# Norms in token halves at the stage boundaries of a two-block transformer kernel

## What is computed

```python
def first_block(...):
    for l in range(2):
        x = _post_norm(x, _swiglu(_modulate(x, sh1, sc1), ...), g1, 0.5, ...)
        x = _post_norm(x, _token_mixer(_modulate(x, sh2, sc2), ...), g2, 1.0, ...)
        x = _post_norm(x, _swiglu(_modulate(x, sh3, sc3), ...), g3, 0.5, ...)

def _post_norm(x, y, gate, res_w, gain, bias):
    return _layer_norm(ALPHA * x + res_w * (1.0 + gate) * y, gain, bias)

def second_block(...):
    for i in range(2):
        x = x + mixer_i(rmsnorm(x, g_mix[i]))
        x = x + cross_attn(rmsnorm(x, g_xattn[i]), rmsnorm(mem, g_mem[i]), ...)
        x = x + square(relu(rmsnorm(x, g_mlp[i]) @ w_up[i])) @ w_down[i]
```

## Time and profile before

| | |
|---|---|
| median of 3 runs | 3772.74 us (3771.07 to 3775.48) |
| the profiled execution | 3767.59 us, span 3766.3 us |
| mean granted TensorE clock | 0.961 of full speed |
| TensorE busy | 3578.6 us, 95% |
| DVE, ACT, POOL busy | 1759.2, 1234.8, 507.3 us |
| DMA | 373.40 MB, 99 GB/s on average |

### The profile page before, as it was taken

One profiled execution on the slowest core, in us unless ns is written; L12 is line 12 of the kernel. 1 busy time (PEld: TensorE's weight loads), 2 busy tenths in 40 slices (PEclk: granted clock), 3 DMA queues, 4 the chain that ended last, 5 costly groups with the idle time before them and its releaser, 6 DMA issues.

```text
span 3766.3 us, 40780 instructions
## 1 busy us (share of the span) xinstructions
PE 3578.6 (95%) x16716; PEld 2898.0 (77%) x16716; DVE 1759.2 (47%) x3072; ACT 1234.8 (33%) x1670; POOL 507.3 (13%) x433
## 2 busy tenths in 40 slices
PE   8999999899998999999899989988999998999999
PEld 7888767678886888767688876746878887787887
DVE  5544553555444544444533234685543333564332
ACT  2222362332223222462332223234442223343222
POOL 1010121110011010121110011111121111202111
PEclk9999899999998999999899998988999999999999
DMA  6443222134432443211122221100212222222222
GB/s 257 166 148 145 102 86 81 56 123 149 164 135 101 155 158 131 83 46 45 50 105 90 100 73 58 66 12 34 90 62 96 101 101 72 99 75 82 101 92 76
DMA packets 52604, 373.40 MB, mean 99 GB/s; under 512 B 5825, under 2 KB 5953, under 8 KB 9538
## 3 DMA queue, kind: packets, MB, share of 16 engines
q1 hardware_dynamic: 52418, 370.79, 27.3%
HBM read 368.67 MB, written 2.10 MB: 98 GB/s over the span
## 4 chain that ended last, share of the span: by engine, by line
PE 86%; DVE 7%; ACT 4%; issue 2%; POOL 1%; DMA 0%; ACTq 0%; DVEq 0%; SPq 0%; POOLq 0%
PE ps L1215 85%; DVE s_wl L1844 1%; ACT s_wh L1537 1%; DVE s_hl L1838 1%; PE ps L1235 0%; DVE s_xr L1932 0%; ACT L1642 0%; DVE s_tmp L2064 0%; DVE s_hh L1938 0%; ACT s_tmp L1673 0%; DVE s_tmp L2054 0%; POOL s_tmp L2340 0%; ACT s_hh L1537 0%; POOL s_hl L2316 0%; DVE s_sm L2062 0%
## 5 line engine op out<-in xcount | busy, mean ns | idle before, releaser
L1215 PE MATMUL ps<-s_hh,s_wh 128*128 128x512 f32 (+1 forms) x2840 | 1138.7, 401 | 59.8 <-DVE s_hl L1838 32.7
L1215 PE MATMUL ps<-s_hl,s_wh 128*128 128x512 f32 (+1 forms) x2840 | 1120.5, 395 | 0.0
L1215 PE MATMUL ps<-s_hh,s_wl 128*128 128x512 f32 (+1 forms) x2840 | 1119.8, 394 | 0.0
L1844 DVE TENSOR_TENSOR s_wl<-s_stage,s_wh 128x2048 fp32r<-128x2048 f32 (+1 forms) x277 | 628.5, 2269 | 721.7 <-ACT s_wh L1537 721.5
L1537 ACT ACTIVATE s_wh<-s_stage 128x2048 fp32r<-128x2048 f32 (+1 forms) x277 | 519.8, 1877 | 732.6 <-PE ps L1215 621.8
L1215 PEld LDWEIGHTS ps<-s_hh,s_wh 128*128 128x128 f32 (+1 forms) x2840 | 541.8, 191 | 203.5 <-issue 68.9
L1215 PEld LDWEIGHTS ps<-s_hh,s_wl 128*128 128x128 f32 (+1 forms) x2840 | 541.1, 191 | 117.5 <-issue 0.2
L1215 PEld LDWEIGHTS ps<-s_hl,s_wh 128*128 128x128 f32 (+1 forms) x2840 | 542.6, 191 | 113.1 <-issue 2.4
L1215 PE MATMUL ps<-s_ah,s_wh 128*128 128x512 f32 x1216 | 474.4, 390 | 0.0
L1215 PE MATMUL ps<-s_ah,s_wl 128*128 128x512 f32 x1216 | 473.2, 389 | 0.0
L1215 PE MATMUL ps<-s_al,s_wh 128*128 128x512 f32 x1216 | 473.1, 389 | 0.0
(11 more groups left out here) (414 smaller groups left out, 3285.9 us busy)
## 6 DMA issues: line engine op xcount, KB each, us to landing
s_stage<-in_w_ada SPq DMA_DIRECT2D x64, 1024.0 KB, 4.8
s_stage<-in_ffn_w_gate SPq DMA_DIRECT2D x44, 1024.0 KB, 4.8
s_stage<-in_ffn_w_up SPq DMA_DIRECT2D x44, 1024.0 KB, 4.8
s_stage<-in_ffn_down SPq DMA_DIRECT2D x32, 1024.0 KB, 4.8
s_stage<-in_w_up SPq DMA_DIRECT2D x32, 1024.0 KB, 4.8
s_stage<-in_down_m SPq DMA_DIRECT2D x32, 1024.0 KB, 4.7
s_stage<-in_w_in SPq DMA_DIRECT2D x24, 1024.0 KB, 4.8
s_stage<-in_ffn_down SPq DMA_DIRECT2D x16, 768.0 KB, 4.2
```

Source lines behind the costliest of these rows:

```text
L1215: return pe.matmul(out, lhs, rhs, start=start, stop=stop, skip_group_check=True)
L1844: dve.tensor_tensor(m.WL[:, ws, 0:n], m.STAGE[:, j % NS, 0:n], m.WH[:, ws, 0:n].bitcast(F32), ALU.subtract).then_inc(*e.up("dve_w", "w.lo" ...
```

## The change

Tokens 0 to 255 are half 0, tokens 256 to 511 half 1.

- `residual` writes the last product of a stage (the last `down` group, `w_out` of the first block, `wo_x`): of its chunks the last two are kept and done for half 0 and then for half 1. The norm of half 0 is a unit whose small steps are put between the pieces of half 1's products by `tick`; what is left of it comes at the end of them.
- `in_halves` writes the next stage's first three chunks: all three for half 0, with half 1's norm in steps between them, then the rest of that norm, and all three for half 1. So three chunks must be split at once: `NW = 3`. The third slot and eight buffers for squares and the like lie in the upper part of SBUF, which the mixers use for themselves; they give it back and take it by `lend` and `reclaim`. There is one set of `s_ah` and `s_al` left.
- `prefetch` splits a weight chunk as soon as the slot and the stage buffer allow, in place of one chunk ahead at a fixed point. At the start two chunks are split ahead of the first modulation, in place of one.
- `ln_x` goes tile by tile, one per piece of a product. The groups of the feed-forwards are 8, 6 and 8. The rate of `w_ada` chunks is 0.85 in the feed-forwards, 0.3 in the first mixer and 0 in the second; the other weights keep their order.
- The even mixer has three chunks in halves (`w_kiwi`, `w_in_e` 7 and 0) and one more (`w_in_e` 1) ahead of the point at which `ki` must be ready. Where a `g_xattn` norm stands, nothing but names changes. The last feed-forward's end has no norm and stays.

```diff
-FFN_GROUPS = [(0, 8), (8, 8), (16, 6)]
+FFN_GROUPS = [(0, 8), (8, 6), (14, 8)]
...
-NW = 2
+NW = 3
...
+    def prefetch(self):
+
+        while self.stream and self.nsplit < len(self.stream) and self.nsplit in self.issued:
+            j = self.nsplit
+            if self.stream[j][2]:
+                if len(self.tmp.busy.intersection(range(6))) > 4:
+                    break
+                self.nsplit += 1
+                self.ada(j, *divmod(self.stream[j][1], 36))
+                continue
+            ws = [w for w in self.spare_w if w in self.allowed]
+            if not ws:
+                break
+            self.nsplit += 1
+            self.split(j, ws[0])
+
...
+        self.prefetch()
...
+        if self.stream:
+            self.wfree[ch.ws] = event
+            self.spare_w.append(ch.ws)
+            self.prefetch()
+
+    def lend(self, *events):
+
+        self.allowed = {0, 1, 2}
+        self.wfree[2] = list(events)
+        self.tmp.ids += UP
+        for i in UP:
...
-            self.add("low", *self.split(0))
-            self.nsplit = 1
+        self.prefetch()
...
+    def in_halves(self, *work, reclaim=False):
+
+        chs = []
+        for s in (0, 1):
+            if s and self.late:
+                self.drain(self.late)
+                self.late = None
+            if s and reclaim:
+                self.reclaim()
+            for i, (name, idx, product) in enumerate(work):
+                if s == 0:
+                    if i == 0 and self.late:
+                        self.active.append(self.late)
+                    chs.append(self.take(name, idx, ada=False))
+                product(chs[i], s, i == 0)
+                if s:
+                    self.release(chs[i], ("proj", self.pid))
+
...
+        def half(s):
+            yield
+            if s:
+                yield from self.wait_ticks(2)
+            mean = self.banks.take()
+            self.add("ln_mean", sid, acc[0], xv, mean, s)
+            if s:
+                self.tmp.free(acc[0], ("ln.mean", sid, 0), ("ln.mean", sid, 1))
+            sq = [self.tmp.take(UP) for _ in range(4)]
+            self.add("ln_sub", sid, xv, mean, sq, s)
+            self.banks.free(mean, ("ln.sub", sid, NT - 1, s))
+            yield from self.wait_ticks(4 + s)
+            var, y = self.held.take(), self.yr.take()
+            self.add("ln_var", sid, sq, var, y, s)
+            for q in sq:
+                self.tmp.free(q, ("ln.var", sid, s))
+            self.held.free(var, ("rs.v", "ln", sid, s))
+            yield from self.wait_ticks(2)
+            rs = self.banks.take()
+            self.add("ln_rs", sid, y, rs, s)
+            self.yr.free(y, ("ln.rs", sid, s))
+            if nxt:
+                for i in range(0, NT, 2):
+                    q = self.tmp.take(UP)
+                    self.add("ln_h", sid, rs, small, hfree[s], hv, q, s, i)
+                    self.tmp.free(q, ("h.lo", hv, i, s), ("h.lo", hv, i + 1, s))
+                    yield
+                self.banks.free(rs, ("ln.sc", sid, NT - 1, s))
+                if s:
+                    self.active.append(scaled())
+                return
+            sq = [self.tmp.take(UP) for _ in range(4)]
+            self.add("ln_last", l, idx, sid, rs, sq, [v + 1 for v in xv], s)
...
+        def scaled():
+            for n in range(NT):
+                self.add("ln_x", sid, n, small, hv, xv[n] + 1)
+                yield
+            self.small.free(small, *both(None, "x", NT - 1, xv[NT - 1] + 1))
...
+            for i, (name, idx, product) in enumerate(work):
+                ch = self.take(name, idx, ada=gi > 0 or i > 2)
+                product(ch, None)
+                self.release(ch, ("proj", self.pid))
...
+                self.residual([(names["down"][gi], l * 4 + c) for c in range(4)], G, 256, "a", av,
+                              gate[-1] if gate else None, norm)
+                continue
...
+    def residual(self, names, kt, nc, x, ver, gate, norm, order=None, reads=False):
...
+        whole = len(names) - 2
...
+        def tile(c, t, s):
+            n = per * c + t
+            b, pid = self.feat(chs[c], kt, nc, t, x, ver, s, order=order)
+            self.upd(n, xv[n], b, pid, gate, s)
+            if n > per * whole or s is None and n:
+                self.total(kind, *total, n - 1, xv, s)
+            return pid
...
+        for s in (0, 1):
+            for c in range(whole, len(names)):
+                if s == 0:
+                    chs.append(self.take(*names[c], ada=False))
+                for t in range(per):
+                    pid = tile(c, t, s)
+                if s:
+                    self.release(chs[c], ("proj", pid))
+            self.total(kind, *total, NT - 1, xv, s)
+            ends.append(("proj", pid))
+            if s == 0:
+                if reads:
+                    self.hfree = ends
+                units = begin(total)
+                self.active.append(units[0])
+        self.drain(units[0])
+        self.late = units[1]
         if gate:
...
-        self.add("m_begin", l)
-        proj(9, "sq", True)
-        proj(10, "sk")
...
+        self.in_halves(("w_kiwi", 0, keys), ("w_in_e", 7, turn_wi), ("w_in_e", 0, feats("qa", 0, 0)), reclaim=True)
+        proj(1, "qa", 2, 4)
...
-        for i, key in enumerate(("qa", "ka")):
-            for c in range(2):
-                proj(2 * i + c, key, 2 * c, 8 * i + 4 * c)
+        for c in range(2):
+            proj(2 + c, "ka", 2 * c, 8 + 4 * c)
...
-            self.rate = 0.62
-            total = self.ffn("swiglu", "f1%d" % l, ffn1, l, FFN_GROUPS, [2, None], "ln")
...
+            self.rate = 0.85
+            self.ffn("swiglu", ffn1, l, FFN_GROUPS, [2, None], then(l, 0, (l, 3, 4)))
+            self.rate = 0.3 if l == 0 else 0
...
+    def ln_x(sid, n, small, hv, v):
+        AG, AB = m.small(small)[:, 16:24], m.small(small)[:, 24:32]
+        e.wait_ge(both(None, "h.hi", hv, n), both(None, "h.q", hv, n))
+        act.activation(m.XR[:, n, :], m.XR[:, n, :], ACT.Identity, bias=AB[:, n:n + 1], scale=AG[:, n:n + 1]).then_inc(
+            *e.half("act_x", None, "x", n, v))
...
         assert at <= self.BIG
+        self.WH[2], at = self.put("wh2", [P, 2048], self.UPPER, F32R)
+        self.WL[2], at = self.put("wl2", [P, 2048], at, F32R)
+        up, at = self.put("up", [P, 8, S], at)
```

More of the change, by code:

```diff
@@ new lines, in take @@
+    def take(self, name, idx, ada=True):
+        if not self.stream:
+            self.order.append((name, idx, False))
+            self.due += self.rate if ada else 0
+            if self.due >= 1 and self.fill:
+                self.due -= 1
+                l, c = self.fill.pop(0)
+                self.order.append(("w_ada", l * 36 + c, True))
+                self.ada(0, l, c)
+            return Chunk(0, 0)
+        self.prefetch()
+        while self.stream[self.taken][2]:
+            self.taken += 1
@@ new lines, in rms_halves, with half, rms_norm @@
+    def rms_halves(self, name, l, total):
+        sid, acc = total
+        rid = self.new()
+        self.hv += 1
+        hv, hfree, xv = self.hv, self.hfree, list(self.xv)
+        def half(s):
+            yield
+            if s:
+                yield from self.wait_ticks(2)
+            yield from self.rms_half(name, l, rid, self.squares(sid, acc, s), hv, hfree, xv, s, acc if s else [])
+        return half(0), half(1)
+    def rms_norm(self, name, l, total, meanwhile):
+        sid, acc = total
+        rid = self.new()
+        st, y = self.held.take(), self.yr.take()
+        self.add("rms_a", rid, self.squares(sid, acc, None), st, y, None)
+        for q in acc:
+            self.tmp.free(q, ("rms.st", rid, 0))
+        self.held.free(st, ("rs.v", "rms", rid, None))
+        meanwhile[0]()
@@ L415, in ffn @@
-            if gi == len(groups) - 1:
-                self.hfree = ("proj", pid)
-            done, s = [], None
+                idx = l * names["n_up"] + g0 // 2 + mi
+                if swiglu:
+                    work.append((names["gate"], idx, first(mi, 2 * mi, av)))
+                    work.append((names["up"], idx, second(mi, 2 * mi, av)))
+                else:
+                    work.append((names["up"], idx, first(mi, 2 * mi, av)))
+            if gi == 0 and self.late:
+                self.in_halves(*work[:3])
+                work = work[3:]
@@ L431, in ffn, with project_out @@
         if gate:
-            self.small.free(gate[-1][0], ("x", NT - 1, self.xv[NT - 1]))
-        return total if mean != "rms" else self.squares(*total)
-    def project_out(self, name, idx0, kt, nc, x, ver, gate, mean, order=None):
-        total, done, per = (self.new(), []), [], nc // P
+            self.small.free(gate[0], *both(None, "x", NT - 1, xv[NT - 1]))
+    def project_out(self, name, idx0, x, ver, order=None):
+        total, kt, per = (self.new(), []), 8, 2
         for c in range(NT // per):
-            ch = self.take(name, idx0 + c, ada=c == 0)
```

(18 more changed lines are left out.)

1150 lines of the change are left out of this document (584 added, 566 removed).

## The result

The changed kernel takes 3807.10 us (median of 4 runs, 3806.63 to 3808.55) against 3774.11 us before in the same comparison (3771.07 to 3776.47): ratio 1.0089, 95% interval 1.0071 to 1.0106. It is **slower by 33 us** where I forecast 24 us faster, and lies 29 us beyond the upper end of my range.

A forecast was written before the change was run, and what follows sets the result against it. It took TensorE, busy 95% of the span, as the bound. Terms -21.6 - 13.3 - 0 - 20.7 - 5 + 2.3 + 26.5 + 9 = -22.8 gave 3744.8, set to 3750 us as median; 8-in-10 range 3712 to 3778.

The forecast's parts named there:

- Halving: On TensorE, 2040 products of 512 columns become 4080 of 256, at 0.013 us each: +26.5 us.
- The start: At the start a second weight split stands ahead of the first modulation on VectorE: +2.3 us.
- T + 16.9: Layer norm: the next stage's first product comes 16.9 us after T, the end of half 0's last product.
- the clock's +9: Slow-clock stretches after waits at the layer norms, taken as half the upper end: +9 us, bounds 0 to +17.
- the stall: TensorE waiting at each plain layer norm: 8.4 us in half 0 and 3.6 in half 1, together 12.0.
- The earlier splits: Weight splits issued earlier were taken as hidden beside other work; without cover each costs 1.90 + 2.28 us.
- the term for the mixers: Fewer w_ada chunks and more products ahead of the ki wait cut TensorE's attention waits: -5 us, bounds 0 and -15.7.
- 1 us of stall: Three RMS norms: half 0's short chain was taken as covered by four or more tiles; 4.9 against 11.8 us each, -20.7 together.
- theory C: From the experiments, not the prediction: the mixers lost their time to new buffer places or new w_ada rates.
- Rival 1: Layer norms: the split between the pairs doesn't bind, each of six is 4.2 us better, 3716 us; chance 0.20.
- Rival 2: Norms: small steps on half the tokens don't shrink, 6 x 4 = 24 us, 3774, no change; chance 0.14.
- Rival 3: Norms: the clock falls at every wait, 15 stretches of 2.9 us, about 3785, slower; chance 0.10.

The follow-up runs named there:

- e7: Kernel before, nothing moved, only the 3648 down-projection matmuls of 512 columns each issued as two of 256: 3823.14 us against 3774.24.
- e6: e3 with w_ada rates 0.75 in feed-forwards and 0.62 in both first mixers, in place of 0.85, 0.3 and 0: 3744.86 us.
- e2: Changed kernel with prefetching switched off in the mixers and cross attention, behind the chunks in halves: 3778.43 us.
- e1: Changed kernel with the weight splits released by a residual's last two chunks issued behind half 0's norm: 3773.10 us.
- e3: Changed kernel with splits held until behind half 0's norm and prefetching off in mixers and cross attention: 3739.66 us, ratio to the kernel before 0.9912.
- e8: Against e3 with one split at the start: the even mixer's second qa chunk moved behind the wait for ki, 3738.28 us beside 3737.16.
- e1b: Changed kernel with only the split released by a residual's very last chunk held until behind half 0's norm: 3784.84 us.

## Why the prediction was wrong

**What held.** Halving: +26.5 forecast, 2040 x 0.0134 = 27.3 by e7. The start: +2.3, measured 2.1. The first product behind the first layer norm: I had T + 16.9; the mean of half 0 starts at 409.8, less one tile of 2.9 is T = 406.9, and the first product came at 423.87, T + 17.0. The second pair, which the sum had at T + 21.7 + 2.3 = T + 24.0, came at T + 23.2. The rates in the two first mixers are worth 5 us or more, by e6.

The boundaries as a whole held as well. I take as the price of a boundary what TensorE spends there beyond its products, these counted at 0.227 and 0.120 us, so that halving is not in it; the numbers come from the starts in the timelines of the two traces:

| boundary | before | after | change forecast | measured |
|---|---|---|---|---|
| four layer norms, each | 24.2, 23.8, 23.3, 24.3 | 19.2, 17.6, 19.6, 17.3 | -3.9 | -5.0, -6.2, -3.7, -7.0 |
| between two feed-forwards | 30.8 | 18.6 | -11.8 | -12.2 |
| last layer norm with RMS norm | 38.6 | 38.5 | +1.5 | -0.1 |
| three RMS norms, each | 12.3, 11.3, 11.7 | 10.4, 4.8, 9.7 | -6.9 | -1.9, -6.5, -2.0 |
| sum | 200.3 | 155.7 | -46.6 | -44.6 |

(The forecast has a sixth of the clock's +9 in each layer norm.) So the nine boundaries together account for only 2 of the 56 us between my sum and the result. Within the five plain layer norms it is right in part by luck: the stall was too large, 12.0 us where TensorE's waits are 6.1 to 8.6, and the clock too small, 1.5 us where products that start 0.21 us apart, as they do at the lower clock, add 2.6 to 3.5.

**What failed, first.** The sentence "The earlier splits, the other order of stages and slots and SP's issue of loads are hidden the same way". I took the cover from a stretch of a feed-forward, where VectorE is half idle and nobody waits for it, and carried it to the mixers, where TensorE waits for VectorE 24 times in the attention alone. I even gave the price without cover, 1.90 + 2.28, and didn't ask where it would be paid. So the term for the mixers was -5, with nothing in it for these splits. e2 prices them at 29 us.

**Second.** The RMS norms. I walked through a layer norm, found the split between the pairs and counted its 4.2 us, and then wrote "so I leave 1 us of stall" for the RMS norms, whose steps stand under the same rule of prefetching. The waits at two of them were 4.42 and 4.52, with a slow stretch behind, and e1 takes 5.5, 1.4 and 5.5 us from the three stretches: 12 us together. By the table above the three gained 10.4 us where the sum had 20.7. I never looked at the order there.

**Third, the even mixer.** From -22.8 to +33.0 are 56 us. The boundaries are 2 of them (the RMS norms 10 worse than forecast, the layer norms 8 better), and the 29 of e2 come on top. Another 12 lie in the attention of the even mixer. From the product that waits for `s_hl` (5.99 us above) to the end of that stretch TensorE has the same 759 matmuls in all kernels, by number and shape; their order differs a little:

```profile
2448.48:2634.70 186.22, 156.21 (x759) 101.97 (x760) 134.70 (x444) 80.19 (x205) 20.83 (x19) 0.83 0.07 23
```
```profile
2456.40:2656.84 200.44, 162.79 (x760) 105.77 (x761) 143.22 (x467) 79.42 (x205) 20.39 (x19) 0.80 0.06 21
```
```profile
2411.72:2610.34 198.62, 164.36 (x759) 107.42 (x760) 145.47 (x468) 80.82 (x206) 20.62 (x19) 0.79 0.06 21
```

These are before, after and e3: 186.2, 200.4 and 198.6 us. All of what e3 still loses in the even mixer is here, with more waits (34 us against 30) and a lower granted clock (0.79 against 0.83), while the rest of the stretch, ahead of it, takes 204.2 us where it took 209.3. The sum had a gain there, "more products ahead of its wait for `ki`". e2 has 198.4 and e8 198.4 as well, so neither the splits nor the place of the `qa` chunk is the cause; it stays open, and the buffer places of theory C are a rival that no run tests. The 13 us that are left of the 56 I can't place. Medians and single traces are mixed in this account, and the two traced executions are 8 us further apart than the medians.

Two slips in the working change nothing: 21.7 + 3 x 2.3 is 28.6 and not 28.8, and the forecast's own range by its terms is 3720 to 3771 and not 3728 to 3768.

**The rivals.** Rival 1 said that the split between the pairs might not bind: it bound at five layer norms and at two of the three RMS norms, and at the last layer norm the split stood in front of the RMS norm's small operations (the wait of 6.51). With both splits held back (e1) 34 us came back, with the last one alone (e1b) 22. Rival 2's outcome was no change, by steps that don't shrink; they shrank (VectorE's subtractions, 0.61 whole, are 2.74 / 8 = 0.34 on half the tokens). Rival 3 had the side right, and the cause wrong in the main: the mean granted clock rose from 0.961 to 0.964. But of its mechanism there was more than my +9 had room for. In the 51 us around the first layer norm the clock is 0.93, about 7 us at 1.2 GHz, where the earlier trace rows had 0.69 in 33 us; at the other five it is 0.88, 0.92, 0.88, 0.91 and 0.76 in 39 to 55 us. So the sign of being wrong that I had named, the clock at 0.5 for more than 6 us, came true at all six, and at none of the three RMS norms (0.94, 1.00, 0.94 in 24 to 30 us):

```profile
409.00:460.00 51.00, 42.39 (x312) 40.67 (x311) 31.82 (x82) 25.62 (x50) 13.95 (x16) 0.93 0.12 43
```

The slower side should have been one mechanism that I had already priced: a split in front of a chain that TensorE waits for.

With both splits moved, the change does what it is for: e3 comes out at 3739.7, 35 us below before. That it is near my 3750 is not a success of the sum: the sum had the 4.2 us of the split in each of six layer norms, and without them it would have said 3725.

## What to carry to other kernels

A prefetch that runs "as soon as the slot is free" isn't free where every engine goes through its list in order: the copy is a block of several microseconds in front of whatever comes next in the queue, and it must be placed where nothing urgent stands behind it. Cover is a property of a stage, not of the program: take it from the row of the stage in which the work will stand. And when one rule of a planner puts a block into one place, list every place in which the same rule applies before pricing the change.
